# A 31-tap depthwise convolution spread over the engines: five chunks packed four taps to a TensorE product, from shifted copies

## The reference

```python
def conformer_conv(h, w_in, b_in, w_dw, b_dw, ln_g, ln_b, w_out, b_out):
    a, g = jnp.split(h @ w_in + b_in, 2, axis=-1)
    u = a * jax.nn.sigmoid(g)
    u = causal_depthwise_conv(u, w_dw) + b_dw      # 31 taps per channel
    u = jax.nn.silu(layer_norm(u, ln_g, ln_b))
    return u @ w_out + b_out
```

## Time and profile before

| | us |
|---|---|
| median of 3 runs (2480.06 to 2482.26) | 2482.22 |
| profiled execution, its time | 2480.3 |
| profiled execution, its span | 2478.5 |
| PE busy in the span | 2175.8 (88%) |
| DVE busy | 693.3 (28%) |
| ACT busy | 326.3 (13%) |
| POOL busy | 121.8 (5%) |

### The profile page before, as it was taken

One profiled execution on the slowest core, in us unless ns is written; L12 is line 12 of the kernel. 1 busy time (PEld: TensorE's weight loads), 2 busy tenths in 40 slices (PEclk: granted clock), 3 DMA queues, 4 the chain that ended last, 5 costly groups with the idle time before them and its releaser, 6 DMA issues.

```text
span 2478.5 us, 22995 instructions
## 1 busy us (share of the span) xinstructions
PE 2175.8 (88%) x8988; PEld 1285.6 (52%) x8988; DVE 693.3 (28%) x1220; ACT 326.3 (13%) x735; POOL 121.8 (5%) x165
## 2 busy tenths in 40 slices
PE   7888899979797899979459999999779499999995
PEld 3476577754575677757334444444266344444442
DVE  1335333320354333337641111111231511111113
ACT  1233000000341000013101111111000011111110
POOL 3100100000101000004300000000000000000000
PEclk9855899989755999989669999999989699999998
DMA  8210577562101677743036999999755179999994
GB/s 242 84 51 1 161 256 264 200 241 85 51 1 63 238 267 251 246 164 136 1 110 253 425 427 427 427 427 427 288 203 212 55 326 423 429 427 428 428 427 181
DMA packets 146861, 604.29 MB, mean 244 GB/s; under 512 B 15569, under 2 KB 73265, under 8 KB 118849
## 3 DMA queue, kind: packets, MB, share of 16 engines
q1 hardware_dynamic: 142368, 588.52, 60.6%
q0 software_dynamic: 4192, 14.23, 2.0%
q10 hardware_dynamic: 192, 0.05, 0.0%
HBM read 601.68 MB, written 1.10 MB: 243 GB/s over the span
## 4 chain that ended last, share of the span: by engine, by line
PE 79%; DVE 10%; issue 3%; DVEq 3%; ACT 2%; DMA 2%; PEld 1%; SPq 0%; another core or an unknown queue 0%; PEldq 0%; ACTq 0%
PE ps L1379 26%; PE ps L605 12%; PE ps L455 7%; PE ps L611 6%; PE ps L1364 5%; PE ps L1349 5%; PE ps L1308 3%; PE ps L548 2%; PE ps L588 2%; DVE qkT L1529 2%; PE ps L562 2%; DMA ring<-in_e_w_up 2%; PE ps L1269 1%; DVEq L1610 1%; PE ps L238 1%
## 5 line engine op out<-in xcount | busy, mean ns | idle before, releaser
L605 PE MATMUL ps<-hT,ring 128*128 128x256 f32 x1408 | 309.9, 381 | 2.1 <-DVE hT L250 2.1
L605 PEld LDWEIGHTS ps<-hT,ring 128*128 128x128 f32 x1408 | 274.7, 196 | 33.3 <-issue 4.0
L1379 PE MATMUL ps<-ring,qkT 128*64 128x512 f32 x1024 | 226.8, 595 | 2.9 <-ACT qkT L1508 2.9
L1379 PE MATMUL ps<-ring,hT 128*64 128x512 f32 x1024 | 226.1, 594 | 3.6 <-DMA ring<-in_e_w_gate 2.0
L1379 PE MATMUL ps<-ring,late 128*64 128x512 f32 x1024 | 226.1, 594 | 2.1 <-ACT late L1496 2.1
L1743 DVE TENSOR_TENSOR qkT<-ps,qkT 128x1024 f32<-128x1024 f32 x32 | 39.2, 1225 | 535.5 <-PE ps L1349 535.5
L455 PE MATMUL ps<-ring,hT 128*128 128x494 f32 x384 | 163.1, 584 | 3.6 <-DVE hT L250 2.1
L611 PE MATMUL ps<-ring,late 128*128 128x512 f32 x352 | 154.7, 592 | 0.0
L1379 PEld LDWEIGHTS ps<-ring,hT 128*64 128x64 f32 x1024 | 72.0, 137 | 153.5 <-issue 146.5
L1379 PEld LDWEIGHTS ps<-ring,late 128*64 128x64 f32 x1024 | 72.8, 137 | 149.8 <-issue 149.8
L238 PE MATMUL ps<-ident,O 128*128 128x128 f32 x160 | 36.1, 417 | 124.2 <-DVE O L1555 71.4
(11 more groups left out here) (324 smaller groups left out, 1984.3 us busy)
## 6 DMA issues: line engine op xcount, KB each, us to landing
ring<-in_e_w_gate SPq DMA_DIRECT2D x64, 2048.0 KB, 15.0
ring<-in_e_w_down SPq DMA_DIRECT2D x64, 2048.0 KB, 13.0
ring<-in_e_w_up SPq DMA_DIRECT2D x64, 2048.0 KB, 16.2
ring<-in_ada_w SPq DMA_DIRECT2D x24, 2048.0 KB, 9.9
ring<-in_w_in SPq DMA_DIRECT2D x12, 1976.0 KB, 15.6
ring<-in_w_gate SPq DMA_DIRECT2D x22, 1024.0 KB, 7.5
ring<-in_w_up SPq DMA_DIRECT2D x22, 1024.0 KB, 9.9
ring<-in_w_down SPq DMA_DIRECT2D x22, 1024.0 KB, 11.5
```

The costliest lines, as they stand in the source:

```text
L605: last = mm(m.ps[:, c, at:at + SEQ], w[:, j, c, :], m.hT[:, j, :], start=(j == 0), stop=(j == KC - 1))
L1379: last = mm(m.ps[x * T:(x + 1) * T, out + n, :], operand[:, j, at + x * T:at + (x + 1) * T], w[x][:, j, n * 512:(n + 1) * 512], start=(j = ...
```

## The change

The convolution is divided anew. DVE keeps chunks 0, 1, 2, and does them in slices: behind each chunk's gating product it takes the next 12 taps of the 93, one tap to a drain, and the last 9 behind chunk 7's. POOL does no chunk. PE does chunks 3 to 7, four taps to a product: a chunk's 128 channels are taken as four groups of 32. For a group g, the tile `rep[n % 2][:, g, :]` holds the group's 32 channels four times, each block of 32 partitions shifted by one more token. A product then contracts over 4 shifts x 32 channels into 32 output partitions, `ps[32g:32g+32]`, and 8 steps cover 32 taps (31 and a zero). So a chunk is 32 products of 128x32 by 256 columns (`packed_taps`), in place of 31 products of 128x128.

The shifted copies are DMAs inside SBUF: 16 for a chunk, each of 32 partitions by 284 elements, 8 issued by SP, 8 by ACT (`copies`), behind the chunk's `glu` and, from the third on, behind the packed products that last read that buffer. The stationary tiles (`tapw`) are built by POOL, one product of 128x1024 for each of the five chunks, from a new constant `fold` and a new load `conv_taps`; POOL waits for all packed products before it issues `expert_rows`. `packed_taps` of chunks 3, 4, 5 stand behind the input products of chunks 5, 6, 7; those of chunk 6 next, then the turning back of chunks 0 to 3, then chunk 7's. `sg2` has three buffers where it had four. The statistics are taken in two parts, each behind the four chunks it reads. The pad is 31 zeros where it was 30. The diff, cut to its core:

```diff
 K_A, K_B = 31, 3
-PAD = K_A - 1
+PAD = K_A
...
-CONV_GROUPS = {1: (0, 1), 7: (3, 4, 5)}
-POOL_CHUNKS = (2,)
-PE_CHUNKS = (6, 7)
-DIAGS = 4
+DVE_CHUNKS, PE_CHUNKS = (0, 1, 2), (3, 4, 5, 6, 7)
+SHIFTS = 4
+STEPS = (K_A + 1) // SHIFTS
+CH = P // SHIFTS
+REP = SEQ + SHIFTS * (STEPS - 1)
+TAPS_BETWEEN = 12
...
-    m.diag = m.O[:].rearrange("p i d -> p (i d)").rearrange("p (g c) -> p g c", c=P)
+    m.fold = sb("fold", [P, CH], F32)
+    o = m.O[:].rearrange("p i d -> p (i d)")
+    m.tapw = [at.rearrange("p (g c) -> p g c", c=CH) for at in (m.late[:, 2272:3296], z[:, 3072:4096], q[:, 8184:9208], o[:, 0:1024], o[:, 1024:2048])]
+    m.rep = [m.late[:, b * 1136:(b + 1) * 1136].rearrange("p (q t) -> p q t", q=SHIFTS) for b in range(2)]
+    m.taps = z[:, 5768:5928].rearrange("p (n g) -> p n g", n=len(PE_CHUNKS))
...
+        if l == 0:
+            pool.wait_ge(m.rows_in, rows_count(1))
+            for n in range(len(PE_CHUNKS)):
+                if n == 1:
+                    pool.wait_ge(m.t["vec_ps"], 1)
+                if n == 3:
+                    pool.wait_ge(m.t["tr2"], KC)
+                wide = [P, SHIFTS * STEPS, CH]
+                nc.gpsimd.tensor_tensor(m.tapw[n], bcast(m.fold[:].unsqueeze(1), wide), bcast(m.taps[:, n, :].unsqueeze(2), wide), ALU.mult).then_inc(m.t["taps"], 1)
+            pool.wait_ge(m.t["dw_ps"], len(PE_CHUNKS))
         expert_rows(l)
-        if l == 0:
-            for c in POOL_CHUNKS:
-                pool.wait_ge(m.t["glu"], c + 1)
-                for k in range(K_A):
-                    if k <= 1:
-                        pool.drain()
-                    w = m.vec[:, c, V_DW + k:V_DW + k + 1]
-                    src = m.upad[:, c, k:k + SEQ]
-                    if k == 0:
-                        nc.gpsimd.tensor_scalar(m.cvT[:, c, :], src, w, m.vec[:, c, V_BDW:V_BDW + 1], ALU.mult, ALU.add)
-                    else:
-                        nc.gpsimd.tensor_scalar(m.pool_tap[:, k % 2, :], src, w, None, ALU.mult)
-                        pool.drain()
-                        last = nc.gpsimd.tensor_tensor(m.cvT[:, c, :], m.cvT[:, c, :], m.pool_tap[:, k % 2, :], ALU.add)
-                last.then_inc(m.t["v_ready"], 1)
...
+    for n, c in enumerate(PE_CHUNKS):
+        sp.wait_ge(m.t["glu"], c + 1)
+        if n >= 2:
+            sp.wait_ge(m.t["dw_ps"], n - 1)
+        for g in range(SHIFTS):
+            for k in range(SHIFTS // 2):
+                sp.dma_start(m.rep[n % 2][k * CH:(k + 1) * CH, g, :], m.upad[g * CH:(g + 1) * CH, c, k:k + REP]).then_inc(m.t[f"rep{n % 2}"], 16)
     experts(0)
...
+            def packed_taps(n):
+                c = PE_CHUNKS[n]
+                pe.wait_ge(t["taps"], n + 1)
+                pe.wait_ge(t[f"rep{n % 2}"], 16 * SHIFTS * SHIFTS * (n // 2 + 1))
+                for step in range(STEPS):
+                    for g in range(SHIFTS):
+                        last = mm(m.ps[CH * g:CH * (g + 1), c % 4, 0:SEQ], m.tapw[n][:, step * SHIFTS + g, :], m.rep[n % 2][:, g, SHIFTS * step:SHIFTS * step + SEQ],
+                                  start=(step == 0), stop=(step == STEPS - 1))
+                last.then_inc(t["dw_ps"], 1)
+            def back(c):
+                for i in range(TILES):
+                    last = nc.tensor.transpose(m.ps[:, 4 + 2 * i + c // 4, (c % 4) * P:(c % 4 + 1) * P], m.cvT[:, c, i * P:(i + 1) * P], m.ident[:])
+                if c % 4 == 3:
+                    last.then_inc(t["back_ps"], 1)
             for c in range(KC):
                 if c == 4:
                     for k in (0, 1):
                     w = [full("a_in", k)[1] for k in (2, 3)]
                 if c >= 4:
                     pe.wait_ge(t["glu"], c - 3)
+                if c == 7:
+                    pe.wait_ge(t["v_act"], 1)
                 at = (c % 4) * P
                 for half in range(2):
                     for j in range(KC):
                         last = mm(m.ps[:, c % 4, half * SEQ:(half + 1) * SEQ], w[half][:, j, at:at + P], m.hT[:, j, :], start=(j == 0), stop=(j == KC - 1))
                 last.then_inc(t["ag"], 1)
+                if c >= 5:
+                    packed_taps(c - 5)
             for k in (2, 3):
                 free(RING["a_in", k][0])
-            pe.wait_ge(t["glu"], KC)
-            for n, c in enumerate(PE_CHUNKS):
-                for k in range(K_A):
-                    g = n * K_A + k
-                    if g % DIAGS == 0:
-                        pe.wait_ge(t["diag"], g // DIAGS + 1)
-                    last = mm(m.ps[:, 4 + n, 0:SEQ], m.diag[:, g % (4 * DIAGS), :], m.upad[:, c, k:k + SEQ], start=(k == 0), stop=(k == K_A - 1))
-                    if g % DIAGS == DIAGS - 1:
-                        last.then_inc(t["diag_used"], 1)
-                last.then_inc(t["dw_ps"], 1)
-            pe.wait_ge(t["v_ready"], KC)
-            for i in range(TILES):
-                for c in range(KC):
-                    dst = m.ps[:, 4 + 2 * i + c // 4, (c % 4) * P:(c % 4 + 1) * P]
-                    last = nc.tensor.transpose(dst, m.cvT[:, c, i * P:(i + 1) * P], m.ident[:])
-                last.then_inc(t["back_ps"], 1)
+            packed_taps(3)
+            pe.wait_ge(t["v_ready"], len(DVE_CHUNKS))
+            pe.wait_ge(t["v_act"], 1)
+            for c in range(4):
+                back(c)
+            packed_taps(4)
+            for c in range(4, KC):
+                pe.wait_ge(t["v_act"], c - 2)
+                back(c)
...
-    def diagonals(group):
-        for g in range(group * DIAGS, min((group + 1) * DIAGS, len(PE_CHUNKS) * K_A)):
-            c, k = PE_CHUNKS[g // K_A], g % K_A
-            last = a(m.diag[:, g % (4 * DIAGS), :], m.ident[:], ACT.Copy, scale=m.vec[:, c, V_DW + k:V_DW + k + 1])
-        last.then_inc(t["diag"], 1)
+    def packed_out(n):
+        c = PE_CHUNKS[n]
+        act.wait_ge(t["dw_ps"], n + 1)
+        a(m.cvT[:, c, :], m.ps[:, c % 4, 0:SEQ], ACT.Identity, bias=m.vec[:, c, V_BDW:V_BDW + 1]).then_inc(t["v_act"], 1)
+    def copies(n):
+        c = PE_CHUNKS[n]
+        act.wait_ge(t["glu"], c + 1)
+        if n >= 2:
+            act.wait_ge(t["dw_ps"], n - 1)
+        for g in range(SHIFTS):
+            for k in range(SHIFTS // 2, SHIFTS):
+                act.dma_start(m.rep[n % 2][k * CH:(k + 1) * CH, g, :], m.upad[g * CH:(g + 1) * CH, c, k:k + REP]).then_inc(t[f"rep{n % 2}"], 16)
 
     norm_act(nc, act, m, t["std2"])
     phase_end(act, m, 1)
                 act.wait_ge(t["ag"], c + 1)
                 if c == 0:
                     act.wait_ge(t["vec"], 1)
-                if c >= 4:
-                    act.wait_ge(t["glu"], c - 3)
-                a(m.sg2[:, c % 4, :], m.ps[:, c % 4, SEQ:2 * SEQ], ACT.Sigmoid, bias=m.vec[:, c, V_BG:V_BG + 1]).then_inc(t["sig"], 1)
-                if c == 2:
-                    act.wait_ge(t["tr2"], KC)
-                    for group in range(4):
-                        diagonals(group)
-            for group in range(4, -(-len(PE_CHUNKS) * K_A // DIAGS)):
-                act.wait_ge(t["diag_used"], group - 3)
-                diagonals(group)
-            for n, c in enumerate(PE_CHUNKS):
-                act.wait_ge(t["dw_ps"], n + 1)
-                a(m.cvT[:, c, :], m.ps[:, 4 + n, 0:SEQ], ACT.Identity, bias=m.vec[:, c, V_BDW:V_BDW + 1]).then_inc(t["v_ready"], 1)
+                if c >= 3:
+                    act.wait_ge(t["glu"], c - 2)
+                a(m.sg2[:, c % 3, :], m.ps[:, c % 4, SEQ:2 * SEQ], ACT.Sigmoid, bias=m.vec[:, c, V_BG:V_BG + 1]).then_inc(t["sig"], 1)
+                if c == KC - 1:
+                    copies(4)
+                if c >= 5:
+                    packed_out(c - 5)
+                if c in PE_CHUNKS[:4]:
+                    copies(c - PE_CHUNKS[0])
+            for n in range(3, len(PE_CHUNKS)):
+                packed_out(n)
...
-        for c in range(KC):
-            dve.wait_ge(t["sig"], c + 1)
-            u = m.upad[:, c, PAD:]
-            if l == 0:
-                stt(u, m.ps[:, c % 4, 0:SEQ], m.vec[:, c, V_BA:V_BA + 1], m.sg2[:, c % 4, :], ALU.add, ALU.mult).then_inc(t["glu"], 1)
-                taps, first, row = K_A, 0, V_DW
-            else:
-                tt(u, m.ps[:, c % 2, SEQ:2 * SEQ], m.sg2[:, c % 2, :], ALU.mult).then_inc(t["glu"], 1)
-                taps, first, row = K_B, PAD - (K_B - 1), V_DWB
-            group = CONV_GROUPS.get(c, ()) if l == 0 else (c,)
-            if not group:
-                continue
-            for k in range(taps):
-                dve.drain()
-                for cc in group:
-                    last = conv_tap(v, m, cc, k, row, first, l == 0)
-                    if l == 0 and k == taps - 1:
+        if l == 0:
+            order = [(c, k) for c in DVE_CHUNKS for k in range(K_A)]
+            for c in range(KC):
+                dve.wait_ge(t["sig"], c + 1)
+                stt(m.upad[:, c, PAD:], m.ps[:, c % 4, 0:SEQ], m.vec[:, c, V_BA:V_BA + 1], m.sg2[:, c % 3, :], ALU.add, ALU.mult).then_inc(t["glu"], 1)
```

(20 more changed lines are left out.)

26 lines of the change are left out of this document (17 added, 9 removed).

## The result

The changed kernel took 2443.23 us, the median of four runs (2437.87 to 2452.4), beside 2481.14 for the kernel before in the same comparison (four runs, 2477.15 to 2482.26). The ratio is 0.9854 with a 95% interval of 0.9821 to 0.9887: 1.5% faster. The forecast was 2443.

The account below looks back on a forecast made before the run. The prediction took DVE's taps to bound the conv stage: -41.8 us for the earlier end and statistics, +4.0 for POOL's tiles, -37.8 from 2480.3, so 2442.5; median put at 2443, range 2436 to 2460.

Parts of the forecast that it names:

- A packed chunk: PE's 64 records for one chunk, four column groups side by side: 3.7 us, bounds 3.5 and 13.95.
- rival 2: PE's packed chunks: weight loads not covered, 5.4 us a chunk, end +6.8 us, 2450 us; chance 0.08.
- The upper bound of 13.95: A packed chunk on PE if its 64 records of 0.218 us do not run side by side.
- DVE's course: DVE's sliced taps keep up with PE's input products, end at 1167.5, off the path by a microsecond.
- POOL's tiles: POOL builds stationary tiles beside DVE's modulation of the input on the path: +4.0 us, bounds 0 and 6.9.
- rival 1: POOL and DVE take strict turns during the modulation: term 6.9 us, 2446 us; chance 0.20.
- The copies: Shifted copies take 7.2 us from release to use; PE idles 2.9 us before chunk 7's packed products.
- rival 4: Copies become the chain: issues at three times 0.53 us give 2469, at 1.15 2452; first case and between, chance 0.09.
- The turning back: PE's transposes of the conv result end at 1177.3 before POOL's +4.0, near 1181 with it; 40.6 us earlier before that.
- The statistics: Behind the conv stage, the first half is done by the turning back's end: saves half of 2.49, 1.2 us.
- The clock: PE's granted clock in the output product and last chunk: set at nothing, bounds -3.0 and +3.7 us.
- Hidden: Later expert and POOL loads stay off the path, with covers of 60 us and 40 us.

Follow-up runs that it names:

- the kernel with the late tiles: The changed kernel with POOL building all five stationary tiles only behind the transposes of the modulated input: 2438.47 us, ratio 0.9839 to the kernel before.
- third unaltered profile: The changed kernel measured once more with no edit, as neighbour of the last three runs: 2439.51 us, ratio 0.984 to the kernel before.
- three buffers: The changed kernel with a third buffer for the shifted copies, so copies of chunks 5, 6, 7 wait for packed products one lot earlier: 2442.04 us.
- the sliced kernel: The kernel before with only DVE's taps of its five chunks put in slices of 12 behind each gating: 2468.64 us, ratio 0.9954.
- held loads: The changed kernel with SP issuing the expert loads only once PE has seen the last chunk's copies land: 2443.36 us, ratio 0.9858 to the kernel before.

## Why the prediction was right

**What bounded the kernel: right.** DVE's taps did, and all that was gained at the turning back arrived at the first expert product (40.16 us there, of which the stage is 37.8). The slices without the packing gain 10.7 us of the stage, the packing with all 93 taps behind the last gating none. How the 37.8 divide between the two when the taps keep the grouping of before is not shown.

**A packed chunk: 3.7 expected, 3.59 from start to start.** Rows 6 and 8 were the right ones to read for whether the groups run side by side. That the size fits is in part luck: the sum took 0.218 a record and full overlap of four. This form alone takes 0.179, so full overlap would be 2.86 us, and four groups reach 3.18 of 4. The two errors cancel. The loads of 32 columns take 110 ns each in the groups by form, at a pace of 3.59 / 64 = 0.056 us a record, so they lie under records and under each other:

```profile
L1276 PEld LDWEIGHTS ps<-late,qkT 128*32 128x32 f32 x64 | 2.0, 110 | 1.5 <-issue 0.3
```

The Trainium skill (TensorEngine Tiling (Array Packing), Restrictions) has column tiling switch fast weight load off; no run here shows whether it did. The 1.7 us a chunk of rival 2 didn't come; whether loads have a part in the 0.73 us above 2.86 is open. The upper bound of 13.95 was mis-sized: in one group a chunk takes 11.43.

**DVE's course: right.** The last tap ended at 1171.8 against the end of chunk 6 at 1173.2, off the path by 1.5 us where I had said one.

**POOL's tiles: +4.0 expected, +3.4 measured, by errors that cancel.** The rest of tile 0 was summed too low: by rows 11 and 12 it is 1085.29 + 2.9 - 1086.50 = 1.7 and not 1.1, so the term should have read 4.6. A tile takes 1.90 us alone, not 2.9: 1024 elements in one instruction cost less than four times 256 (4 x 0.72). And DVE lost not one tile but nearly all that POOL did beside it: 0.3 us of tile 0 and two whole tiles are 4.1 us of POOL's own time, of which DVE lost 3.4. That is close to rival 1, strict turns, with the right tile. The Trainium skill (SBUF — State Buffer, Who interferes with whom) had it so: of the two ends I took a middle, and its rule was the better guide. By the rule and the measured tile of 1.90 the term is an estimate of 4.1; the kernel with the late tiles got the measured 3.4 back.

**The copies: idle 2.9 expected, 1.84 measured.** From the first issue to the last landing it was 6.67 us (1169.36 to 1176.03) and not 7.2: the last issue started 4.75 behind the first where 0.53 each makes 3.7, and it landed 1.92 behind that where I had 3.5. The two errors have opposite signs. For the landing the nearest row of before was a load from HBM; the Trainium skill (DMA: Bandwidth & Descriptors, Anatomy of one DMA) gives a fixed cost of about 2.0 us and 436 GB/s for a DMA that GpSimd issues. By that the estimate for 36,352 bytes is 2.1; these copies come from the other two queues, and their 1.92 lies near it. PE came to the wait 0.5 us later, through a gap of 0.41 ahead of chunk 6. The issues were 0.62, so neither case of rival 4 came. The run in which SP issues all sixteen is its nearest relative: there the copies end two waits, 5.42 and 3.39, but no sigmoid stands behind an issue, so it isn't a test of it.

**The turning back** ended at 1180.86, expected "near 1181"; against the profile of before, less the start's 0.79, the stage gained 37.8 where the sum had 36.6 (40.6 less 4.0); the 1.2 between them are the 0.6 of the tiles, the 1.1 less idle time, and against them the gap of 0.41. The statistics gave exactly their 1.2.

**The clock: set at nothing, gave 1.9.** The output product took 28.08 in this profile. This is not a fixed gain. It took 28.08 in seven of the fourteen profiles and 29.90 to 30.30 in the others, and the granted clock of its first 4 us tells them apart without exception: 1.00 in the seven (here, the third unaltered profile, three buffers, one group, all copies on SP, the sliced kernel, held loads), 0.50 to 0.54 in the others (0.52 before the change). Behind the turning back PE is mostly idle, and in every profile its clock is at half (1.2 GHz) for some of that stretch; in some it is back at full when the output product begins, in others only some 4 us into it. What decides that isn't shown: both kinds occur with the unaltered kernel, and the half-clock kind also where PE hadn't idled for a DMA at all. So the 1.9 are this profile's and not the change's. The 27.5 of the prediction, from 64 records of 0.43, was 0.6 too low for the product at full clock.

**Hidden: right for what waits, incomplete for what it touches.** The first user of the expert loads didn't wait. I looked only at whether loads come too late for the experts, and not at whether they stand too near to the copies. Whether that costs anything stays open; in one profile of three of this kernel a copy behind the first load landed 5.7 us late, with three buffers one landed 2.0 late, and holding the loads changed nothing where it didn't happen.

**The number: in part luck.** The forecast of 2443 meets 2443.23 more closely than its terms met theirs. By its own words it should have been 2442.5 + 1.9 = 2444.4. The terms came out at 37.8, 1.2 and 1.9, so 40.9 where the sum had 37.8, less 0.8 of a later start, and 0.9 more were lost behind the first expert product. And the same kernel was 38, 31 and 41 us under the kernel before in three comparisons. What is confirmed is the range and the course of the stage: 2436 to 2460 holds all fourteen runs. Of their scatter of 16 us the stage's start alone moves by 8 us from profile to profile, and the one late copy made the stage itself 8.3 longer.

## What to carry to other kernels

When one engine's work is moved to another, count what stays behind the last thing that it waits for: 93 of VectorE's taps stood behind the last gating before the change and 9 after it. TensorE's packed products gained nothing while 93 taps stayed there, the slices alone left 71 and gained 10.7 us, and both together gained 38. Packing a depthwise filter as shifted copies times a small diagonal pays if consecutive products go to different column groups (3.59 against 11.43 us for the same products), and if the copies' issues are shared between two queues (all on one cost 6 to 14 us) and start a whole chunk ahead. An engine that was idle is not free: whoever gives GpSimd work beside a VectorE product on the path should price it as turns taken, or move it to where VectorE waits: there the same five tiles cost VectorE nothing.

## What the hardware did that I had not expected

- Products of 128x32 by 256 columns, all in one column group, took 0.179 us a record, less than the 0.218 of a 128x128 record of as many columns.
- The gain of the packing isn't linear: 11.43, 6.20, 3.59 us for one, two, four groups. Only the order of the same products differs.
- Copies of 35.5 KB inside SBUF land 1.9 to 2.0 us behind their issue at the median, sooner than the 8 KB load from HBM in the earlier trace rows; of those that ended a wait the slowest took 2.3, 3.9 and, once, 7.6 us.
- DVE and POOL together: a product of two SBUF operands took DVE 2.8 us on average instead of 1.2 beside POOL's, whose own took 3.94 and 2.88 instead of 1.90.
- The same output product took 28.08 us or about 30, by whether its first 4 us were granted the full clock (1.00) or half (0.50 to 0.54).
